# Attention scores and transposes of two units at every second step, turning four steps behind

## The reference, cut to what matters

```python
sc = jnp.einsum('bhqd,bhkd->bhqk', qi, k)
sc = jnp.where(mask, sc * scale + bias, NEG)
p = jax.nn.softmax(sc, axis=-1)
out = jnp.einsum('bhqk,bhkd->bhqd', p, v)
```

## Time and profile before

| what | value |
|---|---|
| median of 3 runs | 2143.26 us (2142.16 to 2143.68) |
| span of the profiled execution, first to last instruction | 2140.8 us |
| TensorE busy over the span | 2097.3 us (98%) |
| TensorE weight loads | 1757.1 us (82%) |
| VectorE, ScalarE, GpSimd busy | 1180.6, 899.8, 504.1 us |
| fox, chk | about 92 to 192 us and 192 to 292 us |
| mla | about 1592 to 1733 us |

### The profile page before, as it was taken

One profiled execution on the slowest core, in us unless ns is written; L12 is line 12 of the kernel. 1 busy time (PEld: TensorE's weight loads), 2 busy tenths in 40 slices (PEclk: granted clock), 3 DMA queues, 4 the chain that ended last, 5 costly groups with the idle time before them and its releaser, 6 DMA issues. The chain is left out here.

```text
span 2140.8 us, 34365 instructions
## 1 busy us (share of the span) xinstructions
PE 2097.3 (98%) x13883; PEld 1757.1 (82%) x13883; DVE 1180.6 (55%) x2031; ACT 899.8 (42%) x1574; POOL 504.1 (24%) x488
## 2 busy tenths in 40 slices
PE   8999999999999999999999999999999999999998
PEld 7877678988888897867878899899876678899887
DVE  5244546454343455557667678485555646576335
ACT  5454562333232335235444245243566634344231
POOL 4000000100000010211337456382432118363000
PEclk9999999999999999999999999999999999999999
DMA  5312233233333323210023323334342113334321
GB/s 170 98 50 69 60 88 100 70 109 99 98 95 92 99 83 87 79 32 2 3 63 85 112 82 100 99 99 118 79 100 65 51 51 93 94 95 143 99 89 60
DMA packets 341530, 179.64 MB, mean 84 GB/s; under 512 B 44342, under 2 KB 332260, under 8 KB 341372
## 3 DMA queue, kind: packets, MB, share of 16 engines
q1 hardware_dynamic: 339052, 171.54, 28.6%
q0 software_dynamic: 2320, 5.89, 1.0%
HBM read 172.40 MB, written 2.11 MB: 82 GB/s over the span
## 5 line engine op out<-in xcount | busy, mean ns | idle before, releaser
L602 PE MATMUL bank<-act_hi,w_hi 128*128 128x512 f32 (+1 forms) x1568 | 580.5, 370 | 9.5 <-DVE act_lo L1375 2.4
L585 DVE TENSOR_TENSOR w_lo<-w,w_hi 128x1024 fp32r<-128x1024 f32 (+2 forms) x314 | 406.0, 1295 | 317.7 <-ACT w_hi L577 317.3
L604 PE MATMUL bank<-act_hi,w_lo 128*128 128x512 f32 (+1 forms) x1568 | 560.7, 358 | 0.0
L603 PE MATMUL bank<-act_lo,w_hi 128*128 128x512 f32 (+1 forms) x1568 | 560.2, 357 | 0.0
L577 ACT ACTIVATE w_hi<-w 128x1024 fp32r<-128x1024 f32 (+2 forms) x315 | 316.6, 1013 | 294.1 <-PE bank L604 258.8
L602 PEld LDWEIGHTS bank<-act_hi,w_hi 128*128 128x128 f32 x1568 | 296.5, 189 | 63.6 <-issue 16.6
L604 PEld LDWEIGHTS bank<-act_hi,w_lo 128*128 128x128 f32 x1568 | 296.3, 189 | 44.4
L603 PEld LDWEIGHTS bank<-act_lo,w_hi 128*128 128x128 f32 x1568 | 297.0, 189 | 38.0 <-issue 0.7
L602 PE MATMUL bank<-hid_hi,w_hi 128*128 128x512 f32 (+1 forms) x672 | 248.5, 370 | 0.0
L604 PE MATMUL bank<-hid_hi,w_lo 128*128 128x512 f32 (+1 forms) x672 | 247.9, 369 | 0.0
L603 PE MATMUL bank<-hid_lo,w_hi 128*128 128x512 f32 (+1 forms) x672 | 247.9, 369 | 0.0
(11 more groups left out here) (543 smaller groups left out, 3537.3 us busy)
## 6 DMA issues: line engine op xcount, KB each, us to landing
w<-in_ffn_w_gate_up SPq DMA_DIRECT2D x76, 512.0 KB, 3.9
w<-in_w_in SPq DMA_DIRECT2D x41, 512.0 KB, 3.9
w<-in_w_up SPq DMA_DIRECT2D x32, 512.0 KB, 4.1
w<-in_w_down SPq DMA_DIRECT2D x32, 512.0 KB, 3.8
w<-in_ffn_w_down SPq DMA_DIRECT2D x32, 512.0 KB, 4.1
w<-in_even_w_in SPq DMA_DIRECT2D x28, 512.0 KB, 3.8
w<-in_ffn_w_down SPq DMA_DIRECT2D x16, 384.0 KB, 3.5
seven_w<-in_ffn_w_gate_up SPq DMA_DIRECT2D x24, 256.0 KB, 3.2
```

Of the source, the lines that this page charges most:

```text
L585: last = e.tensor_tensor(w_lo[:, at], src, w_hi[:, at].bitcast(F32), ALU.subtract)
L602: e.matmul(s.acc, *first, start=(k == 0), stop=False)
L603: e.matmul(s.acc, *second, start=False, stop=False)
L604: last = e.matmul(s.acc, *third, start=False, stop=(k == kt - 1))
```

## The change

All three attentions take one form: TURN, VALUES, OUT, RING are 4, 5, 6, 4. At every even step TensorE issues the scores of units m and m+1, then the transposes of m-4 and m-3, and then, where due, the value products of m-5. Nothing of attention is left on its list for odd steps. ScalarE and VectorE still have one unit a step. fox and chk get a fourth tile of probabilities, laid over the last output tile of chk. Since two more steps must find room, places in fox and chk are 0.3 instead of 0.315 tile apart, and the later ones of `LAST_PLACES` 0.1035 instead of 0.11.

```diff
-    def __init__(..., before=None, apart=False, turn=2, split=None):
+    TURN, VALUES, OUT, RING = 4, 5, 6, 4
+    def __init__(..., before=None, split=None):
-        self.TURN, self.VALUES, self.OUT, self.RING = turn, turn + 1, turn + 2, turn + 1
...
-    def scores(self, e, n, units):
-        for m in range(n, n + units):
+    def scores(self, e, n):
+        for m in (n, n + 1):
             self.ready(e, m)
             if m >= 2:
                 e.wait_ge(*self.exped.at(m - 1))
-        for m in range(n, n + units):
+        for m in (n, n + 1):
             head, i, keys = self.unit(m)
             e.matmul(self.score[m % 2][:, 0:keys], ...)
...
     def tensor(self, e, a, b):
         for m in self.steps_in(a, b):
-            if m < self.UNITS:
-                if not self.apart:
-                    self.scores(e, m, 1)
-                elif m % 2 == 0:
-                    self.scores(e, m, 2)
-            if 0 <= m - self.TURN < self.UNITS:
+            if m % 2 == 0 and m < self.UNITS:
+                self.scores(e, m)
+            if m % 2 == 0 and 0 <= m - self.TURN < self.UNITS:
                 self.turn(e, m - self.TURN)
+                self.turn(e, m - self.TURN + 1)
             if 0 <= m - self.VALUES < self.UNITS:
                 self.multiply(e, m - self.VALUES)
...
-        probs, probs_T = [core.sb(ctx, "probs", [P, 3, T])], core.sb(ctx, "probs_T", [P, NT + 1, T])
+        probs, probs_T = [core.sb(ctx, "probs", [P, 3, T]), core.alias("probs_last", [P, 1, T], F32, last_at)], core.sb(ctx, "probs_T", [P, NT + 1, T])
...
-    fox = PairAttention(core, bank[2:8], [first + 0.25 + 0.315 * n for n in range(32)], ...
+    fox = PairAttention(core, bank[2:8], [first + 0.25 + 0.3 * n for n in range(32)], ...
-    chk = PairAttention(core, bank[2:8], [second + 0.25 + 0.315 * n for n in range(32)], ..., fox, apart=True)
+    chk = PairAttention(core, bank[2:8], [second + 0.25 + 0.3 * n for n in range(32)], ..., fox)
...
-    mla = PairAttention(..., causal, ready, turn=3, split=split)
+    mla = PairAttention(..., causal, ready, split=split)
...
-LAST_PLACES = [0.5, 0.7, 0.9] + [1.03 + 0.11 * n for n in range(13)]
+LAST_PLACES = [0.5, 0.7, 0.9] + [1.03 + 0.1035 * n for n in range(13)]
```

More of the change, by code:

```diff
@@ L1770, with __init__ @@
     LAST_GROUPS = ((0, 1, 2), (3,))
-    def __init__(self, core, bank, places, queries, keys, values, out, added, ready, before=None, apart=False, turn=2,
-                 split=None):
+    TURN, VALUES, OUT, RING = 4, 5, 6, 4
+    def __init__(self, core, bank, places, queries, keys, values, out, added, ready, before=None, split=None):
         self.core, self.UNITS = core, len(places)
         self.PAIRS = self.UNITS // 8
-        self.TURN, self.VALUES, self.OUT, self.RING = turn, turn + 1, turn + 2, turn + 1
         last, step = places[-1], places[-1] - places[-2]
@@ L1779, in __init__ @@
         self.queries, self.keys, self.values, self.out, self.added, self.ready = queries, keys, values, out, added, ready
-        self.before, self.apart, self.split = before, apart, split
+        self.before, self.split = before, split
         self.score, self.turned, self.o_bank = bank[0:2], bank[2:4], bank[4:6]
@@ L1955, in scalar, with pair_attention_space @@
                 self.split.scalar_step(e, m)
-def pair_attention_space(core, ctx, at=None):
+def pair_attention_space(core, ctx, at=None, last_at=None):
     if at is None:
-        probs, probs_T = [core.sb(ctx, "probs", [P, 3, T])], core.sb(ctx, "probs_T", [P, NT + 1, T])
+        probs, probs_T = [core.sb(ctx, "probs", [P, 3, T]), core.alias("probs_last", [P, 1, T], F32, last_at)], core.sb(ctx, "probs_T", [P, NT + 1, T])
     else:
@@ L3973, in first_attentions @@
     core.ahead = tuple(core.alias(f"ahead_{s}", [P, KD * P], F32R, ahead_at + n * KD * P * 4) for n, s in enumerate(("hi", "lo")))
-    pair_attention_space(core, ctx)
+    pair_attention_space(core, ctx, last_at=o_at + 7 * T * 4)
     core.causal_mask = core.sb(ctx, "causal_mask", [P, T], BF16)
@@ L4024, in first_attentions @@
     first, second = g.start_of(J["chk_q"]), g.start_of(J["gates"])
-    fox = PairAttention(core, bank[2:8], [first + 0.25 + 0.315 * n for n in range(32)], lambda head: qs[0:HD + 1, head, :],
+    fox = PairAttention(core, bank[2:8], [first + 0.25 + 0.3 * n for n in range(32)], lambda head: qs[0:HD + 1, head, :],
                     lambda head: ks[0:HD + 1, head, :], values_of(fox_v), tile_of(o), causal, fox_ready)
-    chk = PairAttention(core, bank[2:8], [second + 0.25 + 0.315 * n for n in range(32)], head_rows(chk_q), head_rows(chk_k), values_of(chk_v),
-                    tile_of(o, 4), near_bias, chk_ready, fox, apart=True)
+    chk = PairAttention(core, bank[2:8], [second + 0.25 + 0.3 * n for n in range(32)], head_rows(chk_q), head_rows(chk_k), values_of(chk_v),
+                    tile_of(o, 4), near_bias, chk_ready, fox)
     g.late = range(first, len(g.subs) - 1)
@@ L4263, in even_out_to_end @@
     mla = PairAttention(core, bank[2:8], places, of_quad(qs), of_quad(ks),
-                        lambda kt, head: v[:, kt, HD * head:HD * head + HD], tile_of(o), causal, ready, turn=3, split=split)
+                        lambda kt, head: v[:, kt, HD * head:HD * head + HD], tile_of(o), causal, ready, split=split)
     split.attention = mla
```

## The result

The changed kernel takes 2196.0 us (median of 4 runs, 2194.8 to 2196.6) against 2142.9: 2.4% slower, ratio 1.0242, 95% interval 1.0229 to 1.0254. The forecast was 2188 us, slower with 0.86.

A forecast was written before the change was run, and what follows sets the result against it. TensorE was taken to bound everything, so every new wait is paid in full. Fox 5.3, chk 6.8, mla 31.3 and clock 1.5 sum to +44.9 on 2143.3, giving 2188 us, range 2155 to 2206.

The forecast's parts named there:

- four quarters: The 32 visits of mla in four parts, with stalls of 7.4, 9.6, 11.5 and 11.2 us, sum 39.7.
- TensorE's work is the same: All attentions: same instructions, gain taken as 0; bound 0.1 us at each visit that goes, 6 us.
- fox, forecast 5.3 of stalls: In fox, weight splits inside pairs 2, 5, 7, 10, 12 make TensorE stall 5.3 us where none is now.
- chk, forecast +6.8: In chk, splits inside pairs 0, 2, 5, 7, 10, 12 stall 7.6 us, less 0.8 lost now.
- mla, forecast +31.3: In mla, stalls of 39.7 us over 32 visits, against about 7.3 and 1.1 lost now.
- plain chains: Uninterrupted time from a visit's scores to the next's: 2.7, 3.6, 5.1, 4.2 us for 128, 256, 384, 512 keys.
- interruptions: Weight splits and epilogues between a pair's two exponentials lengthen the chain; a split is 1.05 us for 1024 columns.
- The clock: Long stalls may bring stretches at half clock, 1.7 us of TensorE's work each; taken as +1.5 us net.
- rival 3: Every long stall brings a slow clock stretch, in fox and chk too: ten more of 1.7, 2205 us; chance 10%.
- One sign: ScalarE's waits for transposes were to shrink; no size given.
- Rival 1: Faster: no scores wait, so mla's 7.3, chk's 0.8 and the half clock's 1.7 go; 2133.5 us, chance 8%.
- Rival 2: Splits and epilogues slip into ScalarE's idle time; mla's stalls 10.1 (+2.8), chk's 0.8 goes; 2145 us, chance 6%.

The follow-up runs named there:

- same place: The changed kernel, but the second unit of a pair has the same place as the first: 2150.8 us, ratio 1.0043.
- the version with chk single: The changed kernel with scores one unit a step in all three attentions and one place for both units of a pair: 2151.1 us, ratio 1.0034.
- single scores, same place: The changed kernel, but fox and mla issue one unit's scores a step and both units of a pair share one place; chk keeps pairs: 2137.7 us, ratio 0.9976.

## Why the prediction was right

**Mechanism.** Scores in pairs ask for the partner's exponential, and TensorE, which has nothing to spare, waits. Shown from both sides: put in alone it makes mla 40.5 us longer, taken out alone it gives 34 of mla's 36.2 and all of fox's 8.7 back. In fox, put in alone, it costs 0.5: there it takes the new places too.

It was right visit by visit. TensorE's idle time behind the six forecast pairs of chk (1.1, 1.7, 1.3, 1.8, 1.4, 0.3) is 1.05, 1.64, 1.25, 1.90, 1.26, 0.23. In mla the four quarters, forecast 7.4, 9.6, 11.5 and 11.2 us, have 6.1, 7.9, 10.0 and 8.6 of it; no visit forecast without a stall has one, and of the others one is far off, the visit of units 56 and 57: forecast 2.0, idle 0.06. Of the 25 waits of over 1 us for probabilities in the three attentions, 23 have a split, an epilogue or a half of the mix's operand between the two exponentials; the two without are in mla, 1.20 and 1.74 us long (1625.44, 1768.10).

**TensorE's work is the same.** Right: 13883 matmuls in both, and fox with merged visits and no waits ("same place") is 0.5 us shorter for 16 visits less, inside the bound of 0.1 us each.

**fox, forecast 5.3 of stalls, measured +8.7.** The waits stand behind the forecast pairs 2, 5, 7, 10 and 12 and nowhere else (0.94, 1.25, 1.27, 1.03 and 0.23 us for 1.0, 1.4, 1.3, 1.2 and 0.4). The pair shown, number 5, has a chain of 5.91 us for 5.9 forecast. Idle 4.7 us, with late loads about 5.5; the rest is the clock. The reason I gave for there being no stall before was half of it: besides the single order, places 0.315 apart let few splits fall badly.

**chk, forecast +6.8, measured +8.4.** Idle 7.4 instead of 0.6, and one slow stretch.

**mla, forecast +31.3, measured +36.2.** Idle for probabilities grew from 5.5 to 32.6, by 27.1. The plain chains and the interruptions are both real: 8.4 and up to 27.8 us of it.

**The clock is the term that was mis-sized.** I put +1.5 net, since the trace of before had shown a slow stretch only behind the wait of 1.84 us, and read from it that shorter waits keep the clock. There are eight more, at 1.7 us of work each up to 13.6, and TensorE's busy time grew by 15.2 with the same matmuls, a little of it late starts behind waits. The stalls, forecast 43.4, came out as 38.0 us of idle time. So the stalls were 5.4 too high and the clock 13.7 too low: together the 8 us between 2188 and 2196. That the total came this close is in part luck, as the two misses have opposite signs. How much of a slow stretch shortens the next stall, and so moves from one term to the other, no run separates. My rival 3 had ten more stretches and 2205; the truth lay between it and the forecast, but not by its rule that every long stall brings one: the waits of 2.67 and 2.46 us, up to 1716.36 and 1746.88, have none behind them within 5 us, and that of 1.03 us has. The Trainium skill (TensorE: Matmul & The Clock Gate, "A second HAM failure mode") tells of a kernel in which frequent small idles between groups of matmuls bring the clock down again and again; the trace agrees here, with nine stretches at waits, the shortest of them 1.03 us (up to 156.77; the stretch begins at 158.95).

**One sign failed.** I expected ScalarE's waits for transposes to shrink. They are fewer, 49 instead of 75, but longer in all; the rows of its copies in the two pages, before and after:

```profile
L1932 ACT ACTIVATE probs_T<-bank 128x128 f32<-128x128 f32 (+3 forms) x128 | 56.0, 437 | 83.2 <-PE bank L1826 66.7
```

```profile
L1930 ACT ACTIVATE probs_T<-bank 128x128 f32<-128x128 f32 (+3 forms) x128 | 55.1, 437 | 111.3 <-PE bank L1826 88.0
```

ScalarE stands 88.0 us for transposes instead of 66.7. This idle time isn't TensorE's, and the forecast sum didn't rest on it.

**The range** was given as from 2155, but the terms named for its low end (mla's stalls halved, 20; switching, 6; no clock, 1.5) lead from 2188 to about 2161 only.

**Rival 1** (faster) was right in one half: with scores of fox and mla taken out of the pair form and one place for a pair, the kernel with transposes four steps behind is 5 us under before. **Rival 2** (only plain chains, 2145) needs interruptions not to fall inside pairs; with the same place, where this is enforced, it is 2150.8.

## What to carry to other kernels

With two buffers, batching two producers moves the wait from the unit before last to the last one, and the depth of the pipeline is gone though no work was added; count the chain from the start of a batch to the next, with what else stands in the helper engines' lists between its two halves, against the bound engine's own work in that time. A place computed for steps also places the weight splits and epilogues between them: give both halves of a batch one place, or see that nothing long falls inside. One place needs the pipeline to be deep enough for it: on the kernel before, with two and three steps, it alone cost 22 us. Where the batch's two halves run side by side on the array, as the 64-row scores of chk do, keep it (12 us there); where they can't, leave the scores single. The best version here has the transposes of two units together, four steps behind; no run shows that this by itself gains.

## What the runs showed of the hardware

Scores of 64 rows cost as much alone as two of them together. In the version with chk single, the two scores of 128 keys in one visit, with six transposes between:

```profile
265.50 0.48 PE L1819 MATMUL bank<-chk_k,chk_q 64*128 64x128 f32 x2
265.92 0.88 PE L1828 MATMUL bank<-ident,probs 128*128 128x128 f32 x6
266.73 0.49 PE L1819 MATMUL bank<-chk_k,chk_q 64*128 64x128 f32 x2
267.14 0.50 PE L602 MATMUL bank<-act_hi,w_hi 128*128 128x512 f32 x1
```

Beside it a 65-row score of 128 keys in fox, in the same execution:

```profile
111.62 0.39 PE L1819 MATMUL bank<-fox_k,fox_q 65*128 65x128 f32 x2
111.84 0.82 PE L1828 MATMUL bank<-ident,probs 128*128 128x128 f32 x6
```

The 64-row score takes 0.42 us up to the transposes (the second 0.41 up to the product), the 65-row one 0.22. Two 64-row scores side by side are busy 0.49 at 237.85 in the earlier trace rows, as long as one here: the second is free. I had taken a pair to be a third cheaper than two single ones, and it is half the price.

For 512 keys, alone in chk, as a pair (from "single scores, same place"), and alone with 65 rows in fox:

```profile
209.53 1.12 PE L1819 MATMUL bank<-chk_k,chk_q 64*128 64x512 f32 x2
210.58 0.44 PE L1828 MATMUL bank<-ident,probs 128*128 128x128 f32 x2
```

```profile
229.45 1.13 PE L1819 MATMUL bank<-chk_k,chk_q 64*128 64x512 f32 x4
230.51 0.44 PE L1828 MATMUL bank<-ident,probs 128*128 128x128 f32 x2
```

```profile
128.07 1.02 PE L1819 MATMUL bank<-fox_k,fox_q 65*128 65x512 f32 x2
128.93 0.38 PE L1828 MATMUL bank<-ident,probs 128*128 128x128 f32 x2
```

From start to start one 64-row score takes 1.05 us, a pair 1.06, a 65-row score 0.86. For 128, 256, 384 and 512 keys the 64-row ones take 0.42, 0.63, 0.84 and 1.05, where 65 or 96 rows take 0.22, 0.43, 0.65 and 0.86. So every 128 keys take about 0.21 us in either form, and a 64-row visit adds a fixed 0.2, paid once whether it holds one score or two side by side. At 128 keys the pair only makes up for it (0.42 against twice 0.22); at 512 it is worth 0.7 us (1.06 against twice 0.86). The traces show where part of it may go: the weight load of the 65-row score starts 0.23 us ahead of its matmul (111.39, 111.62), behind the product before it, and that of the 64-row score only with it (265.50). That this is the cause no run tests. The sum fits chk: 16 second scores alone, at 0.21 us for each 128 keys and 0.2 fixed, are 11.6 us, for the 11.5 measured.

The Trainium skill (TensorEngine Tiling (Array Packing), "The Problem" and "Theoretical Speedup") says that small contractions leave the array underused, and that tiles run together are up to twice as fast for 64 rows; the trace agrees, 24.5 to 13.0 us.

And the clock fell behind waits much shorter than the one that the trace of before had shown: behind 1.25 us in fox, at 122.74, the stretch of 0.51 begins at 124.9. The length of a wait does not decide it: 1.03 us up to 156.77 had such a stretch behind it, while 1.27 us up to 139.00 and 1.64 us up to 220.17 had none.
